# Loading and masking the position biases of the neighborhood attention: 32 transfers inside the gated layer, or four beside the short convolution

## The chip, the cores and the metric

The kernel runs on one core of one Trainium2 chip. The metric is the device time of one execution in microseconds (us). The core's engines each follow their own list of instructions: TensorE (PE in the rows, PEld its weight loads), VectorE (DVE), ScalarE (ACT), GpSimd (POOL) and SyncE (SP, which issues the transfers). They meet only at semaphores.

## The reference

Two blocks of a language model are applied to 256 tokens of width 1024, everything in float32. What matters here is the first half of the second block: a short convolution mixer, a gated layer, and neighborhood attention, whose scores get a learned position bias and a mask.

```python
def short_conv_mixer(h, w_in, conv_w, w_out):
    b_gate, c_gate, u = jnp.split(h @ w_in, 3, axis=-1)
    return (b_gate * depthwise_conv3(c_gate * u, conv_w)) @ w_out

def swiglu(h, w13, w2):                       # the gated layer, 2816 hidden columns
    g, u = jnp.split(h @ w13, 2, axis=-1)
    return (jax.nn.silu(g) * u) @ w2

# neighborhood attention: 16 heads, tokens are 4 rows of 64 columns
s = jnp.einsum('bnqhd,brnkhd->bhnqrk', q_r, k_r).astype(jnp.float32) * scale
bias = rpb[:, dr_idx[None, None, :, None], dc_idx[:, :, None, :]]   # rpb: 16 x 15 x 31
s = jnp.where(mask, s + bias.astype(jnp.float32)[None], neg)
p = jax.nn.softmax(...)
```

The bias of a query and a key depends only on the difference of their rows and of their columns. With queries on the partitions (in reversed column order) and keys along the free axis, a query's biases are windows of 64 numbers out of the table's rows of 31; each partition starts one number later in memory. Numbers of a window outside the 16 columns of the neighborhood are whatever lies there, and the mask adds -1e30 to them.

## The kernel before

All weights go through one ring of three slots. A chunk is 1 MB (128 partitions x 2048 numbers). SyncE loads it into `raw` (`load`, L695), ScalarE rounds it to `ring_hi` (`high`, L1710), VectorE forms the rest `ring_lo = raw - ring_hi` (`low`, L2157), and TensorE multiplies with both parts (48 matmuls in `product_f`, L902; 24 in the down projection, L1096). SyncE may load a slot anew once `ring_lo` of the chunk in it is made; ScalarE may overwrite `ring_hi` once TensorE has used the chunk. `STREAM` gives the order of all chunks; every engine walks through it in the same order.

The stretch that matters, in the order of `STREAM`: `a_b0`, `a_c0`, `a_u0` (four chunks each, the products of the short convolution), `a_out0` (four), `ffn0` (33 chunks: the first gated layer), then `b_q0` and so on, the attention. The gated layer goes in rounds of three chunks: gate columns, up columns, down rows. `mlp_rounds` (L272) gives the rounds: round 0 is written out, then comes a loop that each engine runs from registers, then `mlp_peel(name)` rounds written out again. VectorE's part of a round is `gated` (L2444): the gate product is scaled (`gate_in`, L2455), ScalarE takes its silu, VectorE scales that (L2461), multiplies with the up product (`hid`, L2464) and splits the result (L2471, L2472); the last step raises `hid_ready` by one per round. Between these it makes three `ring_lo`. TensorE's `mlp` waits for `banks_read` (raised by L2464) before the next gate product and for `hid_ready` before the down product.

The position biases: `load_bias` (L718) stands in SyncE's list inside round 0 of `ffn0`, behind that round's down chunk. It waits until the first chunk of `a_out0` is drained, since `na_bias` (16 to 40 KB of the work area) lies over `cu` and `acv` of the convolution. It then issues 32 transfers, one per head and per half of the partitions; each brings 64 partitions x 6 windows of 64 numbers. GpSimd (L1694) waits for all 32, adds the mask to all of `na_bias` in one instruction of 6144 numbers per partition, and raises `bias_masked`. VectorE's `score_rows` (L2761) waits for it before the first scores are put together.

GpSimd's other work is small: for each norm it forms the inverse root (`norm_root`), and where the factor must be spread over tokens, `inv_diag` (L1673).

Of the kernel before, what the change touches and what calls it, by code (L numbers as in the profile page):

```python
# [15 lines left out]

# [2 lines left out]

# [5 lines left out]
P = 128  # L25
# [240 lines left out]

def mlp_peel(name):

    return {"ffn1": 2, "ffn3": 1}.get(name, 0)


def mlp_rounds(eng, name):  # L272
# [42 lines left out]
def build(nc, A, out):  # L315
# [5 lines left out]
    with ctx:  # L321
# [29 lines left out]
        def at(name, shape, offset, dt=f32):  # L351
            size = int(np.prod(shape[1:])) * 4
            assert offset + size <= limit, (name, offset + size, limit)
            return nc.alloc_sbuf_tensor_at(name, shape, dt, offset=work0 + offset)
# [59 lines left out]
        at_inv = [at(f"at_inv{u}", [P, 2, TT], 73 * KB + 96 * u + 64) for u in range(2)]  # L414
        merge_t = at("merge_t", [P, 2, SEQ], 74 * KB)
        NA_SPANS = SEQ // GRID_W + 2
        na_bias = at("na_bias", [P, HEADS, NA_SPANS * GRID_W], 16 * KB)
        na_probs = [at(f"na_probs{b}", [P, 2, TT * SEQ], (40 + 4 * b) * KB) for b in range(2)]
        na_turned = [at(f"na_turned{b}", [P, 2, TT * SEQ], o * KB) for b, o in enumerate((58, 62, 66, 70, 74, 86))]
        q_square = at("q_square", [P, 2, SEQ], 102 * KB)  # L420
# [273 lines left out]
        def _(sp):  # L694
# [20 lines left out]
                                 (qk_gain[0:HD, 1:2], flat(A["b_k_norm_g_2"], 1)), (qk_gain[HD:P, 1:2], flat(A["b_k_norm_g_2"], 1))):  # L715
                    sp.dma_start(dst, src, allow_slow_non_contiguous=True).then_inc(late_tables, 16)

            def load_bias():  # L718

                sp.wait_ge(drained, DRAINED["a_out0"] + 1)
                rpb = A["b_rpb_2"]
                head, row = (2 * NA_ROWS - 1) * (2 * NA_COLS - 1), 2 * NA_COLS - 1
                for h in range(HEADS):
                    for half in range(2):
                        src = bass.AP(rpb.tensor, h * head + (NA_SPANS - 1 - half) * row + NA_COLS - GRID_W,
                                      [[1, GRID_W], [row, NA_SPANS], [1, GRID_W]])
                        dst = na_bias[half * GRID_W:(half + 1) * GRID_W, h, :]
                        sp.dma_start(dst.rearrange("p (a b) -> p a b", b=GRID_W), src).then_inc(bias_loaded, 16)  # L730

            def load_mlp(name, gate, up, down, after_first=None):

# [28 lines left out]
            def load_ffn(layer):  # L762
                w13 = A["f_w13_2"][layer].rearrange("(k p) n -> p k n", p=P)
                w2 = A["f_w2_2"][layer].rearrange("(k p) n -> p k n", p=P)
                load_mlp(f"ffn{layer}", lambda i: w13[:, :, ds(i * COLS, COLS)],
                         lambda i: w13[:, :, ds(i * COLS + FFN, COLS)],
                         lambda i: w2[:, ds(i * 2, 2), :], {0: load_bias, 1: load_hyena_tables}.get(layer))

            sp.dma_start(x[:, :, :], A["x"][0].rearrange("(t p) n -> p t n", p=P)).then_inc(x_loaded, 16)
            sp.dma_start(ident[:, :], A["ident"]).then_inc(ident_loaded, 16)  # L770
# [60 lines left out]
                load_expert("down", step)  # L831
            load_cols("ple_gate", A["w_ple_gate"][0], 0, {2: load_late_tables})
            load_cols("a_b0", A["a_w_in_2"][0], 0)
            load_cols("a_c0", A["a_w_in_2"][0], D)
            load_cols("a_u0", A["a_w_in_2"][0], 2 * D)
            load_cols("a_out0", A["a_w_out_2"][0], 0)
            load_ffn(0)
# [823 lines left out]
        def _(pool):  # L1661
# [23 lines left out]
            for operand in SQUARED[1:]:  # L1685
                norm_root(operand)
                if operand == "mix1":
                    for j in range(KT // 2):
                        pool.wait_ge(eps_added, j + 1)
                        pool.tensor_tensor(rate[:, j, :, :, :].rearrange("p q t h -> p (q t h)"),  # L1690
                                           rate_in[:, j, :, :, :].rearrange("p q t h -> p (q t h)"), neg_half[:, :], POW)\
                            .then_inc(qk_rated, 1)
                if operand == "ffn0":
                    pool.wait_ge(late_tables, 16 * LATE_DMAS)  # L1694
                    pool.wait_ge(bias_loaded, 16 * 2 * HEADS)
                    bias = na_bias[:, :, :].rearrange("p h (s c) -> p (h s) c", c=GRID_W)
                    pool.tensor_tensor(bias, bias, na_mask[:, :].unsqueeze(1).to_broadcast([P, HEADS * NA_SPANS, GRID_W]), ADD)\
                        .then_inc(bias_masked, 1)

        @block.scalar  # L1700
        def _(act):
# [444 lines left out]
        def _(dve):  # L2146
# [613 lines left out]
            def score_rows(i):  # L2760
                b = i % 2  # L2761
                dve.wait_ge(na_scored, i + 1)
                if i == 0:
                    dve.wait_ge(bias_masked, 1)
                if i % 2 == 0:
                    dve.wait_ge(qk_rated, i // 2 + 1)
                if i > 1:
                    dve.wait_ge(na_probs_turned, i - 1)
                for h in range(2):
                    for t in range(TT):  # L2770
                        c = (TT - 2 * t) * GRID_W
                        dve.scalar_tensor_tensor(out=na_probs[b][:, h, t * SEQ:(t + 1) * SEQ], in0=acc[:, h, t * SEQ:(t + 1) * SEQ],
                                                 scalar=rate[:, i // 2, 0, t, i % 2 * 2 + h:i % 2 * 2 + h + 1], in1=na_bias[:, 2 * i + h, c:c + SEQ],
                                                 op0=MUL, op1=ADD).then_inc(na_biased, 1)
                dve.wait_ge(na_biased, 4 * (i + 1))
                dve.tensor_reduce(na_max[b][:, :, :], na_probs[b][:, :, :].rearrange("p h (t k) -> p h t k", t=TT),
                                  AX.X, ALU.max, negate=True).then_inc(na_peaked, 1)
# [320 lines left out]
```

## Time and profile before

| | |
|---|---|
| median of three runs | 2172.4 us (2171.49, 2172.4, 2175.82) |
| profiled execution | 2168.56 us, its span 2166.6 us |
| PE / PEld busy | 1987.0 us (92%) / 1809.2 us (84%) |
| DVE busy | 1397.9 us (65%) |
| ACT busy | 917.8 us (42%) |
| POOL busy | 45.9 us (2%) |
| mean granted clock | 0.957 of full speed |
| chain that ended last | PE 56%, DVE 12%, DMA 5%, ACT 4%, issue 3%, SPq 1% |

The 1.96 us between the span and the profiled execution's own time lie around the first and the last instruction. The profile's overview cuts the span into 40 slices of 54 us; the gated layer in question begins at about 960 us and its attention at about 1175 us. Start times in the rows are us from the span's start. A value in square brackets behind a row is the engine's idle time just before it and who ended it.

### The profile page before, as it was taken

The page shows a single profiled execution, that of the slowest core. Times are in us where ns is not written, and L with a number is a line of the kernel's source. Part 1 is how long each engine was busy: PE and PEld are TensorE (multiplying, and loading weights), DVE is VectorE, ACT ScalarE, POOL GpSimd, SP SyncE. Part 2 cuts the span into 40 slices and gives each one's busy share as a digit, 9 for nine tenths or more (in the row PEclk, how much of TensorE's full clock was granted, in tenths as well). Part 3 has the DMA queues.
Part 4 walks back from the last instruction along what each step waited for, and adds up shares of the span by engine and source line. Part 5 has one row for each costly group of instructions (what it writes and reads, how often), then busy time and mean ns, then how long its engine had stood idle before and what let it go on. Part 6 is the DMA issues. An engine that isn't in the chain of part 4 may idle for free.

```text
span 2166.6 us, 33150 instructions
## 1 busy us (share of the span) xinstructions
PE 1987.0 (92%) x13478; PEld 1809.2 (84%) x13478; DVE 1397.9 (65%) x1579; ACT 917.8 (42%) x980; POOL 45.9 (2%) x58
## 2 busy tenths in 40 slices
PE   7998677889999997985999999998997999999999
PEld 7998455777777777985998999997887999899998
DVE  4566666577677756664656756556898555666665
ACT  4344233366566655342334544333433433433332
POOL 0000000000000001002000100000000000000000
PEclk9989588999999999997999999999999999999999
DMA  6644030177767764555555328554223555554553
GB/s 205 202 137 154 0 102 23 43 281 289 283 256 289 298 223 150 176 148 162 193 194 175 118 86 256 185 188 156 67 90 117 169 180 194 167 177 143 196 192 115
DMA packets 254596, 367.28 MB, mean 170 GB/s; under 512 B 25302, under 2 KB 228649, under 8 KB 242089
## 3 DMA queue, kind: packets, MB, share of 16 engines
q1 hardware_dynamic: 254505, 365.99, 50.5%
q8 instruction: 66, 1.08, 0.2%
q14 instruction: 25, 0.20, 0.0%
HBM read 364.92 MB, written 1.05 MB: 169 GB/s over the span
## 4 chain that ended last, share of the span: by engine, by line
PE 56%; DVE 12%; DMA 5%; ACT 4%; issue 3%; SPq 1%; DVEq 0%; POOL 0%; ACTq 0%
PE proj L902 29%; PE acc L1096 10%; PE proj L921 6%; DMA raw<-in_w_exp_up_dram 5%; PE proj L1279 3%; DVE ring_lo L2157 2%; DVE ring_lo L2614 2%; PE acc L1249 2%; SPq L730 1%; ACT ring_hi L1884 1%; ACT second_hi L1884 1%; ACT ring_hi L1710 1%; DVE second_lo L2614 1%; PE acc L1355 1%; PE acc L1109 1%
## 5 line engine op out<-in xcount | busy, mean ns | idle before, releaser
L2157 DVE TENSOR_TENSOR ring_lo<-raw,ring_hi 128x2048 fp32r<-128x2048 f32 x242 | 562.5, 2326 | 274.4 <-ACT ring_hi L1710 273.8
L1710 ACT ACTIVATE ring_hi<-raw 128x2048 fp32r<-128x2048 f32 x242 | 462.1, 1912 | 552.9 <-PE proj L902 300.6
L902 PE MATMUL proj<-h_hi,ring_hi 128*128 128x256 f32 x1936 | 557.7, 288 | 19.6 <-DVEq L2193 7.7
L902 PE MATMUL proj<-h_lo,ring_hi 128*128 128x256 f32 x1936 | 549.4, 284 | 0.0
L902 PE MATMUL proj<-h_hi,ring_lo 128*128 128x256 f32 x1936 | 549.3, 284 | 0.0
L902 PEld LDWEIGHTS proj<-h_hi,ring_hi 128*128 128x128 f32 x1936 | 372.2, 192 | 30.9 <-issue 20.4
L902 PEld LDWEIGHTS proj<-h_lo,ring_hi 128*128 128x128 f32 x1936 | 372.3, 192 | 2.5 <-issue 1.4
L902 PEld LDWEIGHTS proj<-h_hi,ring_lo 128*128 128x128 f32 x1936 | 372.1, 192 | 0.0
L902 PE MATMUL proj<-g_hi,ring_hi 128*128 128x256 f32 x704 | 197.0, 280 | 27.3 <-DVE hid L2464 27.3
L902 PE MATMUL proj<-g_lo,ring_hi 128*128 128x256 f32 x704 | 196.1, 279 | 0.0
L902 PE MATMUL proj<-g_hi,ring_lo 128*128 128x256 f32 x704 | 195.9, 278 | 0.0
L902 PEld LDWEIGHTS proj<-g_hi,ring_hi 128*128 128x128 f32 x704 | 133.7, 190 | 28.9 <-DVE hid L2464 23.6
L902 PEld LDWEIGHTS proj<-g_lo,ring_hi 128*128 128x128 f32 x704 | 133.7, 190 | 0.8
L902 PEld LDWEIGHTS proj<-g_hi,ring_lo 128*128 128x128 f32 x704 | 133.7, 190 | 0.0
L2614 DVE TENSOR_TENSOR second_lo<-raw,second_hi 128x2048 fp32r<-128x2048 f32 x48 | 109.9, 2292 | 32.2 <-ACT second_hi L1884 32.1
L2614 DVE TENSOR_TENSOR ring_lo<-raw,ring_hi 128x2048 fp32r<-128x2048 f32 x48 | 109.2, 2290 | 25.0 <-ACT ring_hi L1884 24.7
L1784 ACT ACTIVATE silu_g<-gate_in 128x512 f32<-128x512 f32 x44 | 27.8, 632 | 208.5 <-DVE gate_in L2455 208.5
L1884 ACT ACTIVATE second_hi<-raw 128x2048 fp32r<-128x2048 f32 x48 | 92.0, 1917 | 34.7 <-DMA raw<-in_w_exp_up_dram 17.7
L921 PE MATMUL proj<-ring_hi,h_hi 128*128 128x256 f32 x320 | 95.2, 298 | 8.8 <-DVE h_lo L2522 8.0
L1884 ACT ACTIVATE ring_hi<-raw 128x2048 fp32r<-128x2048 f32 x48 | 91.1, 1914 | 24.8 <-DMA raw<-in_w_exp_down_dram 9.6
L1096 PE MATMUL acc<-ring_hi,hid_lo 128*128 128x512 f32 x320 | 99.5, 392 | 0.0
L1096 PE MATMUL acc<-ring_lo,hid_hi 128*128 128x512 f32 x320 | 99.3, 391 | 0.0
(414 smaller groups left out, 3333.5 us busy)
## 6 DMA issues: line engine op xcount, KB each, us to landing
raw<-in_f_w_dram SPq DMA_DIRECT2D x132, 1024.0 KB, 5.1
raw<-in_w_exp_gate_dram SPq DMA_DIRECT2D x32, 1024.0 KB, 4.8
raw<-in_w_exp_up_dram SPq DMA_DIRECT2D x32, 1024.0 KB, 4.8
raw<-in_w_exp_down_dram SPq DMA_DIRECT2D x32, 1024.0 KB, 4.8
raw<-in_w_in_dram SPq DMA_DIRECT2D x29, 1024.0 KB, 5.1
raw<-in_a_w_in_dram SPq DMA_DIRECT2D x24, 1024.0 KB, 5.1
raw<-in_b_w_qkv_dram SPq DMA_DIRECT2D x12, 1024.0 KB, 5.1
raw<-in_c_w_in_dram SPq DMA_DIRECT2D x12, 1024.0 KB, 5.2
```

The lines of the kernel that those rows point to most:

```text
L730: sp.dma_start(dst.rearrange("p (a b) -> p a b", b=GRID_W), src).then_inc(bias_loaded, 16)
L902: last = pe.matmul(bank[:, a, :], w[:, k, a * P:(a + 1) * P], h[:, k, :], start=(k == 0 and w is hi and h is h_h and (a == 0 or not first) ...
L921: last = pe.matmul(bank[:, t, :], h[:, k, t * P:(t + 1) * P], w[:, k, :], start=(k == 0 and w is hi and h is h_h), stop=(k == KT - 1 and h ...
L1096: last = pe.matmul(acc[:, 2 * t + m, :], h[:, k, t * P:(t + 1) * P], w[:, k, m * HALF:(m + 1) * HALF], start=(start and k == 0 and h is hi ...
L1109: last = pe.matmul(acc[:, 2 * t + m, :], h[:, k, t * P:(t + 1) * P], w[:, k, m * HALF:(m + 1) * HALF], start=False, stop=(k == 1 and h is ...
L1249: last = pe.matmul(bank, h[:, k, 0:P], w[:, k, m * HALF:(m + 1) * HALF], start=(first and k == 0 and h is hid_hi and w is hi), stop=(k == ...
L1279: last = pe.matmul(pair(v % RING), h, w, start=(k == 0 and h is h_h and w is hi), stop=(k == KT - 1 and h is h_l))
L1710: act.activation(w_hi[n.slot][:, :], raw[n.slot][:, :], ACT.Copy).then_inc(hi_ready, 1)
L1784: act.activation(silu_g[:, :], gate_in[:, :, :].rearrange("p a n -> p (a n)"), ACT.Silu).then_inc(silu_ready, 1)
L1884: act.activation(dst, raw[c.slot][:, :], ACT.Copy).then_inc(hi_ready, 1)
L2157: dve.tensor_tensor(w_lo[n.slot][:, :], raw[n.slot][:, :], w_hi[n.slot][:, :].bitcast(f32), SUB)\
L2614: dve.tensor_tensor(dst, raw[c.slot][:, :], hi.bitcast(f32), SUB).then_inc(lo_ready, 1)
```

## The change

- `load_bias` takes a number g and issues one transfer: for half of the partitions and eight heads it brings each head's whole run of 219 numbers (876 bytes) that contains the six windows (5 x 31 + 64 = 219), into a new buffer `na_runs` at 64 KB. There are four such transfers.
- The four stand in SyncE's list behind the four chunks of `a_c0`, and wait until the first chunk of `a_b0` is drained. Nothing is left in `ffn0`.
- GpSimd makes `na_bias` from `na_runs` and the mask in eight instructions of 768 numbers per partition, two heads each. The windows are read with a step of 31 numbers. Each waits for `hid_ready` of its own round: the first for two (round 0 of the loop over rounds), the last for nine.
- VectorE waits for `bias_masked` at eight instead of one.
- `mlp_peel("ffn0")` is 1 instead of 0: the last round of `ffn0` is written out on every engine.

```diff
 def mlp_peel(name):
-    return {"ffn1": 2, "ffn3": 1}.get(name, 0)
+    return {"ffn0": 1, "ffn1": 2, "ffn3": 1}.get(name, 0)
...
+        NA_RUN = (NA_SPANS - 1) * (2 * NA_COLS - 1) + GRID_W
         na_bias = at("na_bias", [P, HEADS, NA_SPANS * GRID_W], 16 * KB)
+        na_runs = at("na_runs", [P, HEADS, NA_RUN], 64 * KB)
...
-            def load_bias():
-                sp.wait_ge(drained, DRAINED["a_out0"] + 1)
-                rpb = A["b_rpb_2"]
+            def load_bias(g):
+                sp.wait_ge(drained, DRAINED["a_b0"] + 1)
+                half, first = g % 2, g // 2 * (HEADS // 2)
                 head, row = (2 * NA_ROWS - 1) * (2 * NA_COLS - 1), 2 * NA_COLS - 1
-                for h in range(HEADS):
-                    for half in range(2):
-                        src = bass.AP(rpb.tensor, h * head + (NA_SPANS - 1 - half) * row + NA_COLS - GRID_W,
-                                      [[1, GRID_W], [row, NA_SPANS], [1, GRID_W]])
-                        dst = na_bias[half * GRID_W:(half + 1) * GRID_W, h, :]
-                        sp.dma_start(dst.rearrange("p (a b) -> p a b", b=GRID_W), src).then_inc(bias_loaded, 16)
+                src = bass.AP(A["b_rpb_2"].tensor, first * head + (NA_SPANS - 1 - half) * row + NA_COLS - GRID_W,
+                              [[1, GRID_W], [head, HEADS // 2], [1, NA_RUN]])
+                sp.dma_start(na_runs[half * GRID_W:(half + 1) * GRID_W, first:first + HEADS // 2, :], src).then_inc(bias_loaded, 16)
...
-                         lambda i: w2[:, ds(i * 2, 2), :], {0: load_bias, 1: load_hyena_tables}.get(layer))
+                         lambda i: w2[:, ds(i * 2, 2), :], load_hyena_tables if layer == 1 else None)
...
-            load_cols("a_c0", A["a_w_in_2"][0], D)
+            load_cols("a_c0", A["a_w_in_2"][0], D, {j: functools.partial(load_bias, j) for j in range(4)})
...
-                    pool.wait_ge(bias_loaded, 16 * 2 * HEADS)
-                    bias = na_bias[:, :, :].rearrange("p h (s c) -> p (h s) c", c=GRID_W)
-                    pool.tensor_tensor(bias, bias, na_mask[:, :].unsqueeze(1).to_broadcast([P, HEADS * NA_SPANS, GRID_W]), ADD)\
-                        .then_inc(bias_masked, 1)
+                    pool.wait_ge(bias_loaded, 16 * 4)
+                    for h in range(0, HEADS, 2):
+                        runs = na_runs[:, h:h + 2, 0:GRID_W]
+                        windows = bass.AP(runs.tensor, runs.offset, [runs.ap[0], runs.ap[1], [2 * NA_COLS - 1, NA_SPANS], [1, GRID_W]])
+                        mask = na_mask[:, :].unsqueeze(1).unsqueeze(1).to_broadcast([P, 2, NA_SPANS, GRID_W])
+                        pool.wait_ge(hid_ready, ROUNDS["ffn0"] + h // 2 + 2)
+                        pool.tensor_tensor(na_bias[:, h:h + 2, :].rearrange("p h (s c) -> p h s c", c=GRID_W), windows, mask, ADD)\
+                            .then_inc(bias_masked, 1)
...
-                    dve.wait_ge(bias_masked, 1)
+                    dve.wait_ge(bias_masked, HEADS // 2)
```

SyncE's list before, from the end of the first block to the loop of the gated layer. `a_w_in` holds the twelve chunks of `a_b0`, `a_c0` and `a_u0`, `a_w_out` those of `a_out0`, `f_w_2` those of `ffn0`:

```order
216 L700 DMA raw<-in_w_ple_gate_dram 128x8x256
217 L700 DMA raw<-in_a_w_in_dram 128x8x256 x12
218 L700 DMA raw<-in_a_w_out_dram 128x8x256 x4
219 L700 DMA raw<-in_f_w_2_dram 128x8x256 x4
220 L700 DMA raw<-in_f_w_2_dram 128x2x1024
221 L730 DMA na_bias<-in_b_rpb_dram 64x6x64 x32
222 L279 UNCONDITIONAL_BRANCH
```

And after the change:

```order
217 L704 DMA raw<-in_a_w_in_dram 128x8x256 x5
218 L732 DMA na_runs<-in_b_rpb_dram 64x8x219
219 L704 DMA raw<-in_a_w_in_dram 128x8x256
220 L732 DMA na_runs<-in_b_rpb_dram 64x8x219
221 L704 DMA raw<-in_a_w_in_dram 128x8x256
222 L732 DMA na_runs<-in_b_rpb_dram 64x8x219
223 L704 DMA raw<-in_a_w_in_dram 128x8x256
224 L732 DMA na_runs<-in_b_rpb_dram 64x8x219
225 L704 DMA raw<-in_a_w_in_dram 128x8x256 x4
226 L704 DMA raw<-in_a_w_out_dram 128x8x256 x4
```

The bias transfers move from behind the fifth load of `ffn0` to behind the fifth, sixth, seventh and eighth load of `a_w_in`.

GpSimd's list before, between the norm of the gated layer and the next norm, with the semaphores that each instruction waits for:

```order
31 L1673 TENSOR_TENSOR inv_diag<-ident_sb,inv 128x256 [waits inv_ready]
32 L1697 TENSOR_TENSOR na_bias<-na_bias,na_mask_sb 128x6144 [waits bias_loaded,late_tables]
33 L1668 TENSOR_TENSOR ms<-ssq 128x2 [waits ssq_ready]
```

And after the change:

```order
31 L1675 TENSOR_TENSOR inv_diag<-ident_sb,inv 128x256 [waits inv_ready]
32 L1703 TENSOR_TENSOR na_bias<-na_runs,na_mask_sb 128x768 [waits hid_ready,bias_loaded,late_tables]
33 L1703 TENSOR_TENSOR na_bias<-na_runs,na_mask_sb 128x768 [waits hid_ready] x7
34 L1670 TENSOR_TENSOR ms<-ssq 128x2 [waits ssq_ready]
```

The one long instruction became eight short ones, each tied to a round of the gated layer; what follows on GpSimd is the norm at the layer's end.

## Rows read from the trace of the kernel before

**Rows 1.** Timeline of ScalarE: start us, us, operation, x count [idle before <-releaser]

```profile
996.64 1.91 ACT L1710 ACTIVATE ring_hi<-raw 128x2048 fp32r<-128x2048 f32 x1 [18.93 <-DMA raw<-in_f_w_dram]
```

**Rows 2.** Timeline of VectorE in gated layer 0, rounds 0 to 3

```profile
962.06 0.69 DVE L2455 TENSOR_TENSOR gate_in<-proj,inv_b 128x512 f32<-128x512 f32 x1
...
976.36 0.69 DVE L2455 TENSOR_TENSOR gate_in<-proj,inv_b 128x512 f32<-128x512 f32 x1 [3.98 <-PE proj L902]
998.59 10.51 DVE L2157 TENSOR_TENSOR ring_lo<-raw,ring_hi 128x2048 fp32r<-128x2048 f32 x1 [21.54 <-ACT ring_hi L1710]
...
1017.79 0.69 DVE L2455 TENSOR_TENSOR gate_in<-proj,inv_b 128x512 f32<-128x512 f32 x1 [1.78 <-PE proj L902]
...
1024.09 0.69 DVE L2464 TENSOR_TENSOR hid<-silu_g,proj 128x512 f32<-128x512 f32 x1
...
1029.10 0.69 DVE L2472 TENSOR_TENSOR hid_lo<-hid,hid_hi 128x512 fp32r<-128x512 f32 x1
1030.68 2.29 DVE L2157 TENSOR_TENSOR ring_lo<-raw,ring_hi 128x2048 fp32r<-128x2048 f32 x1 [0.88 <-ACT ring_hi L1710]
1034.19 0.69 DVE L2455 TENSOR_TENSOR gate_in<-proj,inv_b 128x512 f32<-128x512 f32 x1 [1.23 <-PE proj L902]
```

**Rows 3.** Timeline of SyncE's transfers, and their line's summary

```profile
952.51 32.49 SPq L730 DMA_DIRECT2D na_bias<-in_b_rpb_dram x32
L730 SPq DMA_DIRECT2D na_bias<-in_b_rpb_dram x32: 621/786/2822, 952.5 to 984.4; - x32
```

**Rows 4.** Timeline of GpSimd

```profile
958.92 0.61 POOL L1673 TENSOR_TENSOR inv_diag<-ident_sb,inv 128x256 f32<-128x256 f32 x1
993.79 13.15 POOL L1697 TENSOR_TENSOR na_bias<-na_bias,na_mask_sb 128x6144 f32<-128x6144 f32 x1 [34.26 <-DMA na_bias<-in_b_rpb_dram]
```

**Rows 5.** Timeline of VectorE in gated layer 3: its first and last rounds

```profile
1984.67 0.69 DVE L2455 TENSOR_TENSOR gate_in<-proj,inv_b 128x512 f32<-128x512 f32 x1
...
1997.37 0.69 DVE L2455 TENSOR_TENSOR gate_in<-proj,inv_b 128x512 f32<-128x512 f32 x1 [2.38 <-PE proj L902]
...
2013.86 0.69 DVE L2455 TENSOR_TENSOR gate_in<-proj,inv_b 128x512 f32<-128x512 f32 x1 [1.31 <-PE proj L902]
...
2128.66 0.69 DVE L2455 TENSOR_TENSOR gate_in<-proj,inv_b 128x512 f32<-128x512 f32 x1 [1.23 <-PE proj L902]
...
2144.97 0.69 DVE L2455 TENSOR_TENSOR gate_in<-proj,inv_b 128x512 f32<-128x512 f32 x1 [1.14 <-PE proj L902]
```

**Rows 6.** Windows in gated layers 0 and 3; the first line names the columns

```profile
core 0: us, PE busy (x) PEld busy (x) DVE busy (x) ACT busy (x) POOL busy (x), PEclk, DMA share, GB/s
969.00:972.00 3.00, 2.99 (x15) 3.00 (x16) 2.94 (x3) 0.00 (x0) 0.00 (x0) 0.55 0.56 80
1991.60:1994.60 3.00, 2.97 (x26) 3.00 (x27) 2.93 (x3) 0.00 (x0) 0.00 (x0) 1.00 1.02 329
```

**Rows 7.** SyncE, VectorE, ScalarE beside the short convolution; then landing times

```profile
853.72 0.37 SPq L700 DMA_DIRECT2D raw<-in_a_w_in_dram  x1
861.55 0.69 DVE L2181 TENSOR_TENSOR pj<-proj,inv_b 128x512 f32<-128x512 f32 x1
872.59 1.91 ACT L1710 ACTIVATE ring_hi<-raw 128x2048 fp32r<-128x2048 f32 x1 [3.85 <-PE proj L902]
raw<-in_a_w_in_dram SPq DMA_DIRECT2D x24, 1024.0 KB, 5.1
```

**Rows 8.** Windows: within `a_b0`; the bias transfers; one round of layer 0

```profile
873.00:879.00 6.00, 6.00 (x53) 6.00 (x52) 3.23 (x3) 2.15 (x2) 0.00 (x0) 1.00 0.57 185
957.40:982.00 24.60, 22.56 (x179) 22.29 (x179) 10.95 (x10) 8.19 (x8) 1.69 (x4) 0.93 0.67 99
1034.19:1050.59 16.40, 16.40 (x122) 15.41 (x122) 9.97 (x8) 6.28 (x4) 0.00 (x0) 1.00 0.58 192
```

**Rows 9.** Chain of waits in time order: start us, us, what

```profile
1010.47 12.64 PE proj L902 x96
1028.60 10.91 PE proj L902 x96
```

More of the change, by code:

```diff
@@ L18 @@
 from contextlib import ExitStack
+import functools
 import numpy as np
```

## The prediction

> **What bounds the kernel.** The page's table of busy times comes first: TensorE is busy 92% of the span, and the chain that ended last runs through it for 56%. So time is won only where TensorE stands still or runs at the low clock. The timelines of the engines around the bias load show the largest such place. ScalarE waits 18.93 us for a chunk's data [rows 1], VectorE 21.54 us behind it, and its next `ring_lo` then takes 10.51 us where others take 2.29 [rows 2]. From the second `gate_in` of layer 0 to the third 41.43 us pass (976.36 to 1017.79); the next round takes 16.40 (to 1034.19).
>
> The cause is in SyncE's list. It issues the 32 bias transfers from 952.51 for 32.49 us, 1.015 us each [rows 3], and the loads of the next chunks stand behind them. The first of these lands just before 996.64. At 993.79 the last bias number has landed and GpSimd's mask starts, for 13.15 us, until 1006.94 [rows 4]. VectorE's `ring_lo`, started at 998.59, ends at 1009.10, 2.16 us after GpSimd, about the length of such an instruction alone: it stood still until GpSimd was done.
>
> **What the removal gives.** Gated layer 3 is the same code behind the same kind of stage (short convolution, output product, norm, the same operand buffers), without a bias load. From its first `gate_in` to its third: 2013.86 - 1984.67 = 29.19 us [rows 5]. Layer 0 needs 1017.79 - 962.06 = 55.73 us [rows 2]. Difference 26.54 us. From the third `gate_in` on, layer 0 is already in its steady round, so nothing further is owed there. The difference holds everything at this place: the late load, the mask's hold on VectorE, and the first 96 matmuls after the stall, which took 12.64 us instead of 10.91 [rows 9].
>
> One part of the 26.54 us is not the bias. The first interval is 14.30 us in layer 0 and 12.70 in layer 3. In the three microseconds from 969 TensorE's granted clock is 0.55, partly at its level of 1.2 GHz, and 1.00 at the same place of layer 3 (2.4 GHz) [rows 6]. TensorE stood idle some 2 us ahead of it in both, so I hold it for chance whether that idle time costs the clock, and count half of these 1.60 us: 26.54 - 0.80 = 25.7 us.
>
> **The written-out last round.** Layer 3 has one too: its last `gate_in` comes 2144.97 - 2128.66 = 16.31 us after the one before, a round of the loop takes 16.40 [rows 2, 5]. Gain 0.09 us; no more is to be had, since the loop round keeps TensorE busy for all of its 16.40 us [rows 8]. The sum is 25.8 us.
>
> **The four new transfers.** Each puts one issue in SyncE's list and 512 runs of 876 bytes in the queue. Two places count.
> First the wait. Behind the first new transfer stands the load of `a_c0`'s second chunk, issued at 853.72 before. Now it must follow the end of the first `a_b0` drain, 861.55 + 0.69 = 862.24, and an issue of 1.02 us: 863.3 at the earliest, 865.1 with the longest issue seen, 2.82 us [rows 3, 7]. It needs 5.1 us to land [rows 7], and the bias runs lie ahead of it. Load pace beside this stage: in 6 us the queues are busy 0.57 at 185 GB/s, 3.42 us for 1.11 MB, so 3.2 us for a chunk of 1024 rows of 1 KB, 3.1 ns each [rows 8]. Taken at that pace, 512 runs are 1.6 us, so the chunk lands at 863.3 + 5.1 + 1.6 = 870.0. ScalarE, held by TensorE's use of the slot, wants it only at 872.59 [rows 7]: 2.6 us to spare, 0.8 with the longest issue. The three later loads are issued at about their old times, each with some 8 us between landing and use (the ring is three chunks deep), and add 1.6 us each to a queue that is 43% idle.
> The bound on the other side: 12,288 old pieces of 256 bytes took from 952.51 to 993.79, 41.3 us, 3.4 ns each [rows 3, 4]. If a run of 876 bytes cost like the four and a half pieces that it touches, it would be 15 ns, a transfer 7.5 us, the four 30 us; with four loads of 3.2 us that is 43 us against the 22 us of four chunks (5.46 each by [rows 9]), so up to 20 us late. I take no cost: the runs are near in size to the 1 KB rows. The low end is 0, as no row lets this stage run faster.
> The Trainium skill (DMA: Bandwidth & Descriptors, How a descriptor splits into AXI transactions) speaks against the misaligned start of these runs: a transaction must start on a 256-byte boundary, and the bytes fetched ahead of it cost beats. By it a run of 876 bytes takes up to 36 beats where an aligned 1 KB takes 32, an estimate of 1.8 us for a transfer instead of the 1.6 above; the sum stays the same. No row of before has such a run.
>
> **The eight mask instructions.** Per number the old one took 13.15 us / 6144 = 2.14 ns, `inv_diag` 0.61 us / 256 = 2.38 ns [rows 4]. So 768 numbers take 1.64 to 1.83 us. Each starts when `hid_lo` ends (1029.79 in the round of [rows 2]), and ends by 1031.7. VectorE's next instruction is a `ring_lo` with ScalarE's part ready at 1030.68; stopped until 1031.7 it would end at 1033.9 instead of 1032.97. The `gate_in` behind it waits for TensorE until 1034.19 anyway, so the collision of 1 us falls into 1.23 us of idle time. And `gate_in` may be late: `hid` (the product that TensorE's next gate product waits for) ends at 1024.78, TensorE takes that product up at 1028.60 [rows 2, 9], 3.8 us later. Cost 0. The far end: the price doesn't follow the count at all, 13.15 us each (below). GpSimd's norm behind the eight comes a round later, and VectorE's wait for eight signals is met some 40 us before the scores.
>
> **The sum against the clock.** The profiled execution took 2168.56 us, 3.84 below the median of the runs. 2168.56 - 25.8 = 2142.8 for one like it; by the median 2172.4 - 25.8 = 2146.6 us.
>
> **Rivals.**
> A. *The masks reach TensorE a little.* GpSimd reads windows with a step of 31 numbers, for which no row exists; if a piece takes 5 us, `gate_in` and all behind it slip by 3 us per round and some of it eats through the 3.8 us. I price it as the whole 0.9 us per collision, 7.2 us in eight rounds: 2153.8 us. For it: the 10.51 us row shows a full stop. Against it: the cover above.
> B. *The new transfers starve the short convolution.* Between the bound and nothing, say 8 us given back: 2154.6 us. For it: only 2.6 us to spare at one load. Against it: the queue's idle share.
> C. *The load was not what held.* If the chunk loads of layer 0 would be late without the biases too, only the mask's stop goes, 10.51 - 2.29 = 8.2 us: 2164.2 us. Against it: layer 3 has the same loads and no such wait.
> D. *Slower: GpSimd holds VectorE in eight rounds.* If a piece costs what the one instruction did, 13.15 us, VectorE has its 9.97 us of a round [rows 8] only outside it: a round becomes 23.1 us instead of 16.40, eight of them 54 us more, less 25.8: 2200 us. It decides from a piece of 16.40 + 25.8 / 8 - 9.97 = 9.7 us on. For it: one row with a full stop, and eight such meetings instead of one. Against it: two rows of GpSimd, of 256 and of 6144 numbers, both near 2.2 ns a number.
> The Trainium skill (SBUF — State Buffer, Who interferes with whom) has the rule behind A and D: a VectorE instruction with two SBUF inputs and a GpSimd instruction that reads SBUF exclude each other, and the one that starts first keeps the other out to its end. The row at 998.59 agrees with it.
>
> **Chances and range.** Forecast 0.83, A 0.06, B 0.05, C 0.04, D 0.02. The forecast's own range: the clock takes 24.9 to 26.6 us, the three runs of before lie from -0.9 to +3.4 us around the median, so about 2144 to 2151. I widen it by 2 us on either side for other executions than these three, which reaches almost to A and B: 2142 to 2153. A measurement of this kernel tells a change from none at about 0.2%, 4.3 us. The forecast, A, B and most of C are faster by more; for the part of B near its far end and of C that stays within it 0.02; slower 0.02.
>
> **What would show it.** After: no bias transfer past 880 us; `gate_in` of rounds 0 to 2 of layer 0 apart by 12.7 (or 14.3) and 16.5 us; steady rounds of 16.40; eight GpSimd rows of 1.6 to 1.9 us, each behind a `hid_lo`, with a `ring_lo` of 3.2 us beside them; ScalarE's `ring_hi` in `a_b0` and `a_c0` still released by TensorE and never by a DMA; the last round at 16.31. Wrong it is if a row "<-DMA raw" shows up in the short convolution, if the GpSimd rows are over 4 us, or if rounds of layer 0 exceed 16.5 us.

## The result, and the profile after

| | before | after |
|---|---|---|
| median of four runs | 2171.94 us (2169.4 to 2175.82) | 2144.86 us (2141.7 to 2148.53) |
| ratio of the medians | | 0.9874, 95% interval 0.9853 to 0.9896 |
| profiled execution, its span | 2168.56 us, 2166.6 us | 2141.7 us, 2139.9 us |

The change takes 27 us off, between 22.6 and 31.9 us by the interval. The forecast was 25.8 us and 2146.6 us. The page of after:

```profile
span 2139.9 us, 33097 instructions
PE 1982.1 (93%) x13478; PEld 1805.0 (84%) x13478; DVE 1396.8 (65%) x1579; ACT 917.5 (43%) x980; POOL 46.3 (2%) x65
```

TensorE's busy time is nearly what it was (1987.0 us), so the gain is time in which it stood still. TensorE's waits in gated layer 0 show it. The columns are: who waited, for whom, us in total, times, longest. First before (955 to 1177 us), then after (955 to 1150 us):

```profile
PE proj L902 <- DVE hid L2464: 25.3, 2, 23.2
```

```profile
PE proj L904 <- DVE hid L2470: 2.1, 1, 2.1
```

One wait of 23.2 us is gone; the other, about 2 us in round 0, stays. VectorE's timeline of after answers to [rows 2]:

```profile
961.46 0.69 DVE L2461 TENSOR_TENSOR gate_in<-proj,inv_b 128x512 f32<-128x512 f32 x1
...
974.35 0.69 DVE L2461 TENSOR_TENSOR gate_in<-proj,inv_b 128x512 f32<-128x512 f32 x1 [2.58 <-PE proj L904]
...
987.55 3.20 DVE L2163 TENSOR_TENSOR ring_lo<-raw,ring_hi 128x2048 fp32r<-128x2048 f32 x1 [0.80 <-ACT ring_hi L1716]
991.15 0.69 DVE L2461 TENSOR_TENSOR gate_in<-proj,inv_b 128x512 f32<-128x512 f32 x1 [0.40 <-PE proj L904]
...
1007.55 0.69 DVE L2461 TENSOR_TENSOR gate_in<-proj,inv_b 128x512 f32<-128x512 f32 x1 [0.44 <-PE proj L904]
```

The first `gate_in` to the third: 991.15 - 961.46 = 29.69 us instead of 55.73, 26.04 us less. The next round takes 16.40, as before. A `ring_lo` of 3.20 us stands where a mask piece overlaps it, and the idle time ahead of `gate_in` is down to 0.40 us from 1.23, still released by TensorE. GpSimd's timeline answers to [rows 4], with one piece behind each `hid_lo`:

```profile
986.92 1.68 POOL L1703 TENSOR_TENSOR na_bias<-na_runs,na_mask_sb 128x768 f32<-128x768 f32 x1 [27.99 <-DVE hid_lo L2478]
1003.23 1.72 POOL L1703 TENSOR_TENSOR na_bias<-na_runs,na_mask_sb 128x768 f32<-128x768 f32 x1 [14.63 <-DVE hid_lo L2478]
```

The spans differ by 26.7 us. This is where they lie, each part from start times of rows of the same instruction:

| stretch | before | after | difference |
|---|---|---|---|
| span's start to the second `ring_hi` of `a_b0` | 866.83 | 864.99 | -1.84 |
| from there to the first `gate_in` | 95.23 | 96.47 | +1.24 |
| first to third `gate_in` | 55.73 | 29.69 | -26.04 |
| the last round | 16.40 | 16.31 | -0.09 |

The first line is code that the change doesn't touch. The second looks like a cost of the new transfers, but ten kernels below have 95.1 to 95.3 there, four of them with the very same transfers, so it isn't the transfers; the granted clock is 0.96 of full speed in the stretch against 0.98 before, and I put it down to that, which isn't shown further. Of the third line 1.1 us is that this execution shows no clock drop at the layer's start (see why the prediction was right).

Beside the short convolution SyncE's timeline (answering to [rows 3]), the time from issue to landing of the four, and ScalarE's timeline (to [rows 7]) read:

```profile
860.42 0.65 SPq L732 DMA_DIRECT2D na_runs<-in_b_rpb_dram  x1
861.12 0.62 SPq L704 DMA_DIRECT2D raw<-in_a_w_in_dram  x1
861.78 0.62 SPq L732 DMA_DIRECT2D na_runs<-in_b_rpb_dram  x1
863.08 0.37 SPq L704 DMA_DIRECT2D raw<-in_a_w_in_dram  x1
863.49 3.21 SPq L732 DMA_DIRECT2D na_runs<-in_b_rpb_dram  x1
869.25 0.37 SPq L704 DMA_DIRECT2D raw<-in_a_w_in_dram  x1
869.67 2.51 SPq L732 DMA_DIRECT2D na_runs<-in_b_rpb_dram  x1
```

```profile
DMA to landing us min/median/max: 4.9/11.2/14.9
```

```profile
870.75 1.91 ACT L1716 ACTIVATE ring_hi<-raw 128x2048 fp32r<-128x2048 f32 x1 [3.85 <-PE proj L904]
876.51 1.91 ACT L1716 ACTIVATE ring_hi<-raw 128x2048 fp32r<-128x2048 f32 x1 [3.85 <-PE proj L904]
882.38 1.92 ACT L1716 ACTIVATE ring_hi<-raw 128x2048 fp32r<-128x2048 f32 x1 [3.96 <-DMA raw<-in_a_w_in_dram]
```

Two issues block SyncE for 3.21 and 2.51 us, and a transfer takes up to 14.9 us to land; the last of the four lands at 884.6. The chunk loads issued between and behind them take 7.2, 10.5, 13.0, 12.3 and 9.3 us to land, where those of before take 5.0 to 5.8 here. One `ring_hi` is released by its load, 5.87 us after the one before it instead of 5.76: 0.1 us late, with no wait of TensorE behind it.

### The profile page after: what moved, and what is told of

The parts are those of the page before. It is cut to its first block, busy times and chain, and to the rows that moved or that the text cites. A ratio compares the mean times of both kernels' runs of the same rounds, so it can differ in the third digit from the quotient of the medians.

```text
span 2139.9 us, 33097 instructions
## 1 busy us (share of the span) xinstructions
PE 1982.1 (93%) x13478; PEld 1805.0 (84%) x13478; DVE 1396.8 (65%) x1579; ACT 917.5 (43%) x980; POOL 46.3 (2%) x65
## 4 chain that ended last, share of the span: by engine, by line
PE 57%; DVE 12%; DMA 5%; ACT 4%; issue 3%; DVEq 0%; POOL 0%; ACTq 0%
PE proj L904 30%; PE acc L1098 10%; PE proj L923 7%; DMA raw<-in_w_exp_up_dram 5%; PE proj L1281 3%; DVE ring_lo L2163 2%; DVE ring_lo L2620 2%; PE acc L1251 2%; ACT ring_hi L1890 1%; ACT second_hi L1890 1%; ACT ring_hi L1716 1%; DVE second_lo L2620 1%; PE acc L1111 1%; PE acc L1357 1%; PE acc L948 1%
## 5 line engine op out<-in xcount | busy, mean ns | idle before, releaser
L904 PEld LDWEIGHTS proj<-h_hi,ring_hi 128*128 128x128 f32 x1936 | 372.9, 193 | 32.5 <-issue 21.8
```

Source lines behind the costliest of these rows:

```text
L904: last = pe.matmul(bank[:, a, :], w[:, k, a * P:(a + 1) * P], h[:, k, :], start=(k == 0 and w is hi and h is h_h and (a == 0 or not first) ...
```

## The experiments

Each median stands beside that of before, timed on the same chip, with the ratio and its interval. In the edits `...` stands for code left out, and what only follows from an edit (the counts waited for, the number of heads in a mask) is left out too. "Layer" is the time from the first to the last `gate_in` of gated layer 0: 186.93 us before, 160.80 after. In most kernels below TensorE falls to the low clock in the first interval of the layer, which is 14.3 us then instead of 12.7 to 12.9; their undisturbed layer is 161.9.

**1. The old transfers at the new place.** Eight of the 64 x 6 x 64 transfers behind each chunk of `a_c0`, the masks in eight.

```diff
-                src = bass.AP(..., [[1, GRID_W], [head, HEADS // 2], [1, NA_RUN]])
-                sp.dma_start(na_runs[half * GRID_W:(half + 1) * GRID_W, first:first + HEADS // 2, :], src)
+                for h in range(4 * g, 4 * g + 4):
+                    for half in range(2):
+                        src = bass.AP(..., [[1, GRID_W], [row, NA_SPANS], [1, GRID_W]])
+                        sp.dma_start(...)
```

> The changed kernel, but with the 32 old transfers of 64 x 6 windows in place of the four of whole runs: eight behind each chunk of a_c0, into a buffer of their own at 50 KB; the eight masks as in the change. Theory (the place alone is not enough, the whole runs are needed): an issue takes 1.015 us, so SyncE is held 8.1 us per chunk where TensorE needs a chunk each 5.76 us, and 12,288 pieces at 3.4 ns hold the queue 41 us; the loads of the second to fourth chunk of a_c0 and the first of a_u0 come late, TensorE loses 7 to 10 us in the short convolution, the time is 2152 to 2156 us; gated layer 0 as after the change (29.2 to 30.8 us from its first gate_in to its third). Rival (only the place counts, the ring's slack hides any form): 2145 us, no ring_hi row of a_c0 or a_u0 released by a DMA for more than 1 us.

Measured: 2171.88 against 2171.7 us, ratio 1.0002 (0.9987 to 1.0017). The whole gain is gone; I had the direction, and under half of the size. SyncE's list and ScalarE's timeline:

```profile
876.56 11.93 SPq L734 DMA_DIRECT2D na_runs<-in_b_rpb_dram  x8
888.53 0.61 SPq L704 DMA_DIRECT2D raw<-in_a_w_in_dram  x1
889.19 12.37 SPq L734 DMA_DIRECT2D na_runs<-in_b_rpb_dram  x8
901.60 1.77 SPq L704 DMA_DIRECT2D raw<-in_a_w_in_dram  x1
```

```profile
900.49 1.91 ACT L1717 ACTIVATE ring_hi<-raw 128x2048 fp32r<-128x2048 f32 x1 [11.03 <-DMA raw<-in_a_w_in_dram]
913.62 1.91 ACT L1717 ACTIVATE ring_hi<-raw 128x2048 fp32r<-128x2048 f32 x1 [11.22 <-DMA raw<-in_a_w_in_dram]
```

Eight issues take 12 us here, 1.5 us each, and a chunk load gets through once in 13 us where the product wants one each 5.76. From the second `ring_hi` of `a_b0` to the first `gate_in` 121.61 us pass instead of 95.23: +26.4 us, as much as the layer gave. TensorE's waits for `ring_lo` are 19.7 us of it. So moving the old transfers is worth nothing. Beside experiment 3, which has the same transfers and the same eight masks at the old place and takes 2163.63 us, the move costs 8 us.

**2. The new transfers at the old place.**

```diff
-                sp.wait_ge(drained, DRAINED["a_b0"] + 1)
+                sp.wait_ge(drained, DRAINED["a_out0"] + 1)
-  ..., load_hyena_tables if layer == 1 else None)
+  ..., {0: load_all_bias, 1: load_hyena_tables}.get(layer))     # the four, one behind the other
```

> The changed kernel, but the four whole-run transfers stand at the old place, in round 0 of gated layer 0 behind the down chunk, and wait for the first drain of a_out0; eight masks, last round written out. Theory (the form is enough): the four were some 9 us of queue time beside the convolution (2048 runs at 70 ns over 16 queues), so the load behind them is issued by about 959 us and lands by about 968, ahead of the 976 at which ScalarE wants it; first to third gate_in 29.2 to 30.8 us, time 2145 us. Rival (the place is needed: every transfer in front of these loads reaches TensorE): 5 us or more lost in that stretch, 2150 us or more.

Measured: 2146.0 against 2171.7 us, ratio 0.9882 (0.9848 to 0.9917), with the interval of the whole change inside it. So the new form, with the eight masks, brings the gain at the old place too, and the move adds nothing that can be told. The group of four issues, and a window in which only these transfers move (columns as in [rows 6]):

```profile
955.08 2.81 SPq L736 DMA_DIRECT2D na_runs<-in_b_rpb_dram x4
```

```profile
961.00:967.00 6.00, 6.00 (x52) 5.95 (x51) 3.36 (x3) 3.82 (x4) 1.03 (x2) 1.00 1.13 203
```

The issues take 2.81 us instead of 32.49. The queues are full (1.13) at 203 GB/s: a transfer holds 64 x 8 x 876 bytes = 448 KB, 2.2 us at that pace. I had taken 1.6.

**3. The old load with the mask in eight pieces.** Only the long hold is taken away.

```diff
-                    bias = na_bias[:, :, :]...
-                    pool.tensor_tensor(bias, bias, ...).then_inc(bias_masked, 1)
+                    for h in range(0, HEADS, 2):
+                        bias = na_bias[:, h:h + 2, :]...
+                        pool.wait_ge(hid_ready, ROUNDS["ffn0"] + h // 2 + 2)
+                        pool.tensor_tensor(bias, bias, ...).then_inc(bias_masked, 1)
```

> The kernel before with one edit: the mask is added in place in eight instructions of two heads, each behind its round's hid_ready, as in the change; the 32 transfers stay where they were. Theory (both halves counted: the late loads and the mask's hold of VectorE): ScalarE still waits some 19 us for its chunk, the ring_lo behind it takes 2.3 us instead of 10.5, the first to third gate_in shrink from 55.7 to 47.5 us, time 2164 us. Rival 1 (the mask's hold was covered by the loads that were late anyway): under 3 us gained, 2169 us or more. Rival 2 (the mask was the whole of it): 30 us in that stretch, 2145 us.

Measured: 2163.63 against 2171.7 us, ratio 0.9966 (0.9947 to 0.9984). The layer is 7.44 us shorter. ScalarE's and VectorE's rows at the stall, and TensorE's wait:

```profile
998.73 1.91 ACT L1712 ACTIVATE ring_hi<-raw 128x2048 fp32r<-128x2048 f32 x1 [17.98 <-DMA raw<-in_f_w_dram]
1000.67 2.29 DVE L2159 TENSOR_TENSOR ring_lo<-raw,ring_hi 128x2048 fp32r<-128x2048 f32 x1 [20.59 <-ACT ring_hi L1712]
```

```profile
PE proj L902 <- DVE hid L2466: 16.1, 2, 14.1
```

`ring_lo` takes its own 2.29 us, not 10.51 [rows 2], and the wait of 23.2 us is 14.1. The late load is nearly as late as it was: its `ring_hi` starts 33.7 us behind the first `gate_in`, 34.6 before. Of the 26 us, 7 to 8 are the mask's hold; the rest, by difference, is the loads behind the 32 issues.

**4. The new load with the mask in one piece**, of 6144 numbers, behind round 1.

```diff
-                    for h in range(0, HEADS, 2):
+                    for h in range(0, HEADS, 16):
```

> The changed kernel with one mask instruction of all 16 heads (6144 numbers per partition) behind the second hid_ready, instead of eight of two heads. Theory (GpSimd keeps VectorE out for its whole instruction, and only what exceeds VectorE's 1.2 us and TensorE's 3.8 us of cover costs): it starts near 987 and ends near 1000; the ring_lo ready at 987.6 ends near 1002.2, gate_in comes 11 us late, hid too, TensorE loses 7 us once: 2152 us. Rival (a mask costs nothing wherever it stands once the loads are in time): 2145 us, ring_lo under 4 us.

Measured: 2152.63 against 2171.7 us, ratio 0.9914 (0.9883 to 0.9945); the layer is 169.05 us, 7.1 over its undisturbed length. GpSimd, VectorE, and TensorE's waits:

```profile
991.57 12.28 POOL L1703 TENSOR_TENSOR na_bias<-na_runs,na_mask_sb 128x6144 f32<-128x6144 f32 x1 [29.10 <-DVE hid_lo L2478]
992.19 13.80 DVE L2163 TENSOR_TENSOR ring_lo<-raw,ring_hi 128x2048 fp32r<-128x2048 f32 x1 [0.79 <-ACT ring_hi L1716]
```

```profile
PE acc L1098 <- DVE ring_lo L2163: 4.9, 1, 4.9
PE proj L904 <- DVE hid L2470: 2.1, 1, 2.1
```

The 2.29 us instruction ends 13.80 us after its start, 11.5 us late. TensorE waits 4.9 us for it, in the down projection (`acc`), so its cover is 11.5 - 4.9 = 6.6 us; the other 2.2 us of the layer come at the low clock behind the wait (granted 0.50 from 1004 to 1008 us). The theory had the 3.8 us of the gate product as the cover. No wait shows there: `gate_in` is 10.1 us late, but TensorE is by then 7.1 us late itself, and the 3.0 us between them are covered.

**5 and 6. Two and four pieces** (`range(0, HEADS, 8)` and `range(0, HEADS, 4)`), one execution each.

> The changed kernel with two mask instructions of eight heads each (3072 numbers per partition, 6.6 us), behind the second and third hid_ready. Theory (full hold, cover of 1.2 + 3.8 us): the ring_lo beside each takes 8 us instead of 2.3, the gate_in behind it comes 4.5 us late, TensorE loses 0 to 1 us for each, so rounds of 16.4 to 17.4 us. Rival (a cover of the 1.2 us alone, since all that follows in the round slips too): 4.5 us lost for each, rounds of 20.9 us.

> The changed kernel with four mask instructions of four heads each (1536 numbers per partition, 3.3 us), behind the second to fifth hid_ready. Theory (full hold, cover of 1.2 + 3.8 us): the ring_lo beside each takes 4.8 us, gate_in comes 1.3 us late, TensorE loses nothing: rounds stay at 16.40 us. Rival (cover of 1.2 us alone): 1.3 us lost for each, rounds of 17.7 us.

Measured: 2143.79 us with a layer of 162.45, and 2147.63 us with a layer of 161.90. Four pieces of 3.2 us make a `ring_lo` of up to 4.7 us and `gate_in` 1.0 us late, and TensorE loses nothing. Two pieces cost 0.5 us of the layer. The first makes its `ring_lo` 7.77 us long, 5.5 us late; `gate_in` comes 4.1 us late, and TensorE waits for `hid` at the gate product:

```profile
PE proj L904 <- DVE hid L2470: 0.3, 1, 0.3
```

That is the cover of 3.8 us of the prediction, used up by 0.3 us. The second piece shows the hold from the other side, with GpSimd's and VectorE's rows:

```profile
988.19 6.25 POOL L1703 TENSOR_TENSOR na_bias<-na_runs,na_mask_sb 128x3072 f32<-128x3072 f32 x1 [29.07 <-DVE hid_lo L2478]
1007.03 8.26 POOL L1703 TENSOR_TENSOR na_bias<-na_runs,na_mask_sb 128x3072 f32<-128x3072 f32 x1 [12.59 <-DVE hid_lo L2478]
```

```profile
1006.87 2.28 DVE L2163 TENSOR_TENSOR ring_lo<-raw,ring_hi 128x2048 fp32r<-128x2048 f32 x1
1009.38 0.69 DVE L2461 TENSOR_TENSOR gate_in<-proj,inv_b 128x512 f32<-128x512 f32 x1 [0.23 <-PE proj L904]
1012.65 4.79 DVE L2163 TENSOR_TENSOR ring_lo<-raw,ring_hi 128x2048 fp32r<-128x2048 f32 x1 [2.59 <-ACT ring_hi L1716]
```

The `ring_lo` that started 0.16 us ahead of GpSimd takes its 2.28 us, and GpSimd's instruction is 2.0 us longer than its twin. The next `ring_lo` starts inside it and takes 4.79 us. The one that starts first goes through.

**7. No transfers at all**: `na_runs` is filled with zeros, so the biases are missing from the scores.

```diff
-            load_cols("a_c0", ..., {j: functools.partial(load_bias, j) for j in range(4)})
+            load_cols("a_c0", ...)
```

> The changed kernel without the four bias transfers; GpSimd fills their buffer with zeros once the first drain of a_b0 is done, so the biases are left out of the result and only the mask is in it. Theory (the transfers are hidden beside the short convolution): same time as the changed kernel within 1 us, 2145 us; the a_c0 chunk that waited for a DMA until 882.4 is released by TensorE again. Rival (they cost something there, by the clock or by late loads): 1 us or more faster, and a shorter stretch from the first drain of a_b0 to the first of a_out0.

Measured: 2142.32 against 2170.34 us, ratio 0.9868 (0.9851 to 0.9885). After has 0.9874: what the transfers cost is under what can be told.

**8. Each transfer twice**, the first copy into a spare buffer.

```diff
-                sp.dma_start(na_runs[...], src)
+                for dst in (na_spare, na_runs):
+                    sp.dma_start(dst[...], src)
```

> The changed kernel with each bias transfer issued twice, the second time into a spare buffer. Theory (the cover beside the short convolution is nearly used up: one load landed 0.1 us after ScalarE wanted it, the queues were over 100% busy from 863 to 878 us): 9 us more of queue time, one or two loads 5 to 10 us late at ScalarE, of which chunks made ready 5 to 7 us ahead of TensorE's use take most: TensorE loses 1 to 5 us. Rival (plenty of cover left): no ring_hi of a_c0 or a_u0 more than 1 us late, and no time lost.

Measured: 2154.8 against 2170.34 us, ratio 0.9919 (0.9899 to 0.9939), some 10 us behind after and 12.5 behind experiment 7, timed beside it, where I had expected 1 to 5. The first `ring_hi` released by their loads, and TensorE's wait for them:

```profile
877.00 1.91 ACT L1718 ACTIVATE ring_hi<-raw 128x2048 fp32r<-128x2048 f32 x1 [4.06 <-DMA raw<-in_a_w_in_dram]
887.13 1.91 ACT L1718 ACTIVATE ring_hi<-raw 128x2048 fp32r<-128x2048 f32 x1 [8.22 <-DMA raw<-in_a_w_in_dram]
899.13 1.91 ACT L1718 ACTIVATE ring_hi<-raw 128x2048 fp32r<-128x2048 f32 x1 [10.09 <-DMA raw<-in_a_w_in_dram]
```

```profile
PE proj L906 <- DVE ring_lo L2165: 3.6, 1, 3.6
```

The stretch takes 101.42 us instead of the 95.23 of most kernels. That is 6.2 us; the profiled execution is 13.2 us longer than that of after and has 6.0 of them ahead of the stretch, in code that is the same in both, and 1.1 by the clock in the layer. The profiled execution of experiment 9, with only four transfers, is late by more ahead of the stretch, so that part speaks of chance. Four transfers are free, and the rows of the stretch show that eight are not; how much of the 10 us the other four cost beyond its 6.2 stays open.

**9. A round pitch in the buffer**: each run at a multiple of 896 bytes.

```diff
-        na_runs = at("na_runs", [P, HEADS, NA_RUN], 64 * KB)
+        na_runs = at("na_runs", [P, HEADS, 224], 64 * KB)
```

> The changed kernel with the runs laid 224 numbers (896 bytes) apart in na_runs instead of 219 (876 bytes); the sources are the same, each partition's one number further. It asks why the four transfers took up to 14.9 us to land. Theory (the misaligned start in DRAM): landings as in the changed kernel, 5 to 15 us, queues over 100% busy from 863 to 878 us. Rival (the misaligned start in SBUF): landings 3 to 5 us shorter and no ring_hi of a_c0 released by a DMA. The time is that of the changed kernel by either, 2145 us.

Measured: 2144.41 against 2170.8 us, ratio 0.9875 (0.9857 to 0.9894); landing 5.0/11.4/15.2 us (shortest, median, longest). The pitch does nothing. Its stretch takes 95.23 us with the same four transfers, and that clears them of the +1.24 us above.

**10. Without the written-out last round.**

```diff
-    return {"ffn0": 1, "ffn1": 2, "ffn3": 1}.get(name, 0)
+    return {"ffn1": 2, "ffn3": 1}.get(name, 0)
```

> The changed kernel with the last round of gated layer 0 back in the loop. Theory: the interval between its last two gate_in is 16.40 us instead of 16.31, nothing else changes: 0.1 us, not to be told by the clock. Rival (the written-out round saves a jump or a fetch at the loop's end): 0.5 us or more lost between the last gate_in of the layer and its first x_res.

Measured: 2147.58 against 2170.8 us, ratio 0.9899 (0.9878 to 0.9921), which overlaps that of after. The last two `gate_in` and what follows the layer:

```profile
1107.24 0.69 DVE L2461 TENSOR_TENSOR gate_in<-proj,inv_b 128x512 f32<-128x512 f32 x1 [0.45 <-PE proj L904]
1123.64 0.69 DVE L2461 TENSOR_TENSOR gate_in<-proj,inv_b 128x512 f32<-128x512 f32 x1 [1.23 <-PE proj L904]
1138.72 1.28 DVE L2246 TENSOR_TENSOR x_res<-x_res,acc 128x512 f32<-128x512 f32 x2
```

16.40 and 15.08 us, where after has 16.31 and 15.09. The edit is worth 0.09 us by the profile; the 2.7 us between the medians isn't at this place.

**11. Aligned runs**: every run starts at a multiple of 256 bytes in DRAM (the biases are other numbers).

```diff
-                src = bass.AP(..., first * head + ..., [[1, GRID_W], [head, HEADS // 2], [1, NA_RUN]])
+                src = bass.AP(..., 0, [[64, GRID_W], [320, HEADS // 2], [1, NA_RUN]])
```

> The changed kernel with the sources of the four transfers laid so that every run of 876 bytes starts at a multiple of 256 bytes in DRAM (partitions 64 numbers apart, heads 320); the biases in the result are other numbers of the table. It asks why a transfer of runs costs the queues some 2.2 us beside nothing else (438 KB at 203 GB/s) where chunk rows of 1 KB would make it 1.6. Theory (the misaligned start of each run): queue share from 863 to 878 us down from 1.10 to about 0.85 to 0.95, longest landing 10 us or less instead of 14.9, no ring_hi of a_c0 released by a DMA. Rival (the number of runs, or writing only 64 partitions): share and landings as in the changed kernel. Time 2145 us by either.

Measured: 2144.11 against 2168.74 us, ratio 0.9882 (0.9808 to 0.9956, from two executions). Landing is 4.5/12.6/15.9 us, no shorter than the 4.9/11.2/14.9 of after, the queues are as full (1.11 at 268 GB/s from 862 to 877 us), and three `ring_hi` are released by their loads. The start of a run isn't what makes these transfers slow.

**12. All 128 partitions**: four transfers of 128 partitions x 4 heads, as many runs and bytes (the upper half of the partitions gets other numbers).

```diff
-                              [[1, GRID_W], [head, HEADS // 2], [1, NA_RUN]])
+                              [[1, P], [head, HEADS // 4], [1, NA_RUN]])
```

> The changed kernel with each of the four transfers writing 128 partitions x 4 heads instead of 64 x 8: the same number of runs and bytes, the same misaligned starts; the biases of the upper half of the partitions are other numbers of the table. Theory (the misaligned start is what costs): landings and queue share as in the changed kernel, 5 to 15 us and 1.10. Rival (a transfer to 64 partitions is slower than one to 128): longest landing 10 us or less, share under 0.95. Time 2145 us by either.

Measured: 2145.63 against 2168.74 us, ratio 0.9889 (0.9816 to 0.9962, from two executions). The landing times, then a window of 15 us over the four transfers and its densest part:

```profile
DMA to landing us min/median/max: 4.3/8.5/9.9
```

```profile
864.18:879.18 15.00, 15.00 (x128) 15.00 (x127) 6.69 (x6) 5.34 (x3) 0.00 (x0) 1.00 1.06 336
866.00:872.00 6.00, 6.00 (x52) 6.00 (x52) 3.08 (x3) 2.01 (x2) 0.00 (x0) 1.00 1.10 352
```

The same kind of window of after, and the one of experiment 7 without these transfers:

```profile
863.00:878.00 15.00, 15.00 (x128) 15.00 (x127) 6.71 (x6) 5.32 (x3) 0.00 (x0) 1.00 1.10 283
```

```profile
863.00:878.00 15.00, 15.00 (x127) 15.00 (x126) 7.25 (x6) 5.74 (x3) 0.00 (x0) 1.00 0.60 203
```

The queues are as full, and they move 336 GB/s instead of 283. The longest landing falls from 14.9 to 9.9 us, and every `ring_hi` is released by TensorE. The share of 1.06 isn't what I had named for this rival (under 0.95), the landings are. So what made the transfers slower than I had taken them is that each writes to only 64 partitions. The time stays where it is, since after had lost nothing to it.

## Why the prediction was right

**The removal, 25.7 us: right.** Layer 3 as the measure of layer 0 held to half a microsecond: forecast 29.19 us with no clock drop, 30.80 with one; measured 29.19 in experiment 1, 29.69 in after and 30.80 in experiment 2. For the first two intervals, 12.7 or 14.3 and 16.5 us, after shows 12.89 and 16.80. The second is over the 16.5 us that the prediction named as a sign of being wrong. It is no wait: behind the wait of round 0, at a granted clock of 1.00 in both, 12 of TensorE's matmuls take 1.41 us in after and 1.36 in experiment 1, for some 15 us. Why stays open; the steady rounds are 16.40.

**The clock, -0.80 us: right as a chance.** In after the drop is absent from layer 0 and present in layer 3, whose first interval is 14.41 us, with the code of both unchanged there. That was luck: of the fourteen profiled executions (before, after and the twelve experiments) twelve have it in layer 0 and eight in layer 3, so half was too low a chance for layer 0. With the drop the layer is 161.9 us, and the change's own gain 25.0 us. Of the 26.7 us between the spans 1.1 us are the drop that after lacks and 0.6 the code elsewhere, so part of the closeness to 25.8 is chance; the 25.0 lie within the interval of the medians (22.6 to 31.9 us).

**The cause, two in one place: right, and now divided.** The rival that the load was not what held (C, 2164.2 us) describes the part that experiment 3 removes, 2163.63 us; what it leaves is the late load. The collision of experiment 4 confirms it with the load out of the way.

**Masks at no cost: right.** 1.68 to 1.73 us a piece (forecast 1.64 to 1.83), `ring_lo` 3.03 to 3.20 us (3.2). The Trainium skill (SBUF — State Buffer, Who interferes with whom) says that the two engines exclude each other and that the one in possession goes on to its end; the rows of experiment 4 (`ring_lo` 13.80 us) and of experiment 5 (GpSimd's piece 8.26 us instead of 6.25) agree, on both sides. Rivals A and D fall with it: a piece of twice the length (experiment 6) is still free, and the price begins between 6144 / 4 and 6144 / 2 numbers a piece. The 3.8 us of cover at the gate product are borne out by experiment 5: 4.1 us late, 0.3 us waited. The prediction left out the down product, whose cover is 6.6 us (experiment 4); a piece of growing length meets the gate product's first.

**The transfers at no cost: right in sum, mis-sized in the term.** The step that failed is "load pace beside this stage ... taken at that pace, 512 runs are 1.6 us": the pace of 128-partition rows was applied to 64-partition runs. Measured are 2.2 us (experiment 2), and I had looked for the strain at one load, while it adds up over the four: the queues that were to be partly idle are full (1.10 from 863 to 878 us), the issues grew to 3.21 us, the load issued at 869.25 took 13.0 us to land, and the row that would prove me wrong, a "<-DMA raw" in the short convolution, does stand in after. It cost 0.1 us of ScalarE's time (0.4 to 0.7 in experiments 4, 6 and 10, which have the same transfers) and none of TensorE's; experiment 7 shows the whole as free, and experiment 8 that twice as much isn't. Rival B would have come true with less cover than there was, and did with the old form of the transfers (experiment 1). The misaligned start, which the Trainium skill (DMA: Bandwidth & Descriptors, How a descriptor splits into AXI transactions) charges with extra beats, doesn't show in transfers into 64 partitions: experiment 11 takes it away and lands no sooner.

**The last round, 0.09 us: right** (experiment 10).

Two bounds of the forecast's own range are summed a little low, 24.9 for 25.03 and 2144 for 2144.9; nothing hangs on them.

## What to carry to other kernels

Count a small strided transfer by its issue, not its bytes: 32 of them held the queue's other loads for 32.5 us inside the gated layer and for 42 us beside the convolution, while four transfers of whole runs, with 1.8 MB instead of 3.1, took 2.8 us of issue in the one place and 7.0 in the other, and cost nothing measurable in either; change the form first, and the place matters little. That the issues and not the pieces hold is read from rows, not tried: an issue of 384 pieces took 1.015 us and one of 512 runs 0.63 to 0.70 (experiment 2), and beside the 32 the queues were 0.67 busy [rows 8]. No run has few issues with many pieces.

Cut a long GpSimd instruction that runs beside VectorE's two-input ones until what it holds up has slack enough behind it. Here a `ring_lo` ahead of a gate product could come some 5.0 us late (1.2 us of VectorE's idle time and 3.8 of TensorE's cover): pieces of 3.2 us made it 2.4 us late and cost nothing, pieces of 6.25 us made it 5.5 us late and cost 0.5 us.

## What the runs showed of the hardware

Transfers into 64 partitions run at 203 GB/s with full queues (experiment 2). Those into 128, with runs of the same 876 bytes and 1 MB loads among them, run at 336 to 352 GB/s with queues as full (experiment 12); loads alone have 329 [rows 6]. The Trainium skill (SBUF — State Buffer, Door 1: The DMA port swizzle (why `[64,N]` ≈ `[32,N]`)) says that partitions 0 to 63 reach only half of SBUF's ports, with 196 GB/s for 1 MiB; the 203 GB/s here agree. I hadn't thought of it, and the loads behind such transfers land later too, in 7.2 to 13.0 us instead of 5.0 to 5.8. A further surprise is the issue: the same kind of 64 x 6 x 64 transfer took SyncE 1.015 us each in a row [rows 3], and up to 1.5 us each on the mean of a group of eight, with 1 MB loads between the groups (experiment 1).
